# Raw tokens turned by half tiles, the inverse root behind the first product, and 16 places for expert weights

## The reference

```python
def rms_norm(x, gain):                      # eps 1e-6; rmsnorm(x, g) of the second block is the same
    xf = x.astype(jnp.float32)
    y = xf * lax.rsqrt(jnp.mean(xf * xf, axis=-1, keepdims=True) + EPS)
    return (y * gain.astype(jnp.float32)).astype(x.dtype)

def hier_moe(t, ...):                       # combine: (tokens, 32) weights, two of a row not zero
    for e in range(N_EXPERTS):
        he = jax.nn.silu(t @ w_gate[e]) * (t @ w_up[e])
        y = y + combine[:, e:e + 1] * (he @ w_down[e])

def swiglu(x, w_in, w_out):                 # D_FF = 2816
    gate, up = jnp.split(x @ w_in, 2, axis=-1)
    return (jax.nn.silu(gate) * up) @ w_out
```

## Time and profile before

| | us |
|---|---|
| median of three runs | 1882.8 |
| the runs | 1882.4, 1882.8, 1884.54 |
| the profiled execution | 1881.33 |
| its span in the trace | 1879.5 |
| PE busy in it | 1821.9 (97%) |
| DVE busy in it | 935.5 (50%) |
| ACT busy in it | 734.3 (39%) |
| POOL busy in it | 103.5 (6%) |

### The profile page before, as it was taken

The page is one execution under the profiler, slowest core; times in us unless marked ns, Lnnn a source line. Parts: engine busy times, 40 slices in busy tenths (PEclk is TensorE's granted clock), DMA queues, the critical chain, the costliest instruction groups (busy, mean ns, idle before and its releaser), DMA issues.

```text
span 1879.5 us, 30178 instructions
## 1 busy us (share of the span) xinstructions
PE 1821.9 (97%) x11760; PEld 1439.0 (77%) x11760; DVE 935.5 (50%) x1310; ACT 734.3 (39%) x1167; POOL 103.5 (6%) x113
## 2 busy tenths in 40 slices
PE   5999999999999989999999999999999999999999
PEld 3976644444434379999899998899999998879998
DVE  4873222222222165546878776554555545755554
ACT  2353212212212144444555554444444444754443
POOL 1010000000000000000212211000000000210000
PEclk9999999999999999999999999999999999999999
DMA  9876789999999976665554563566656665036653
GB/s 387 320 258 254 291 335 421 422 422 422 422 422 422 421 224 180 189 184 167 157 149 121 134 165 103 149 186 185 183 168 182 186 188 223 1 90 181 199 174 116
DMA packets 317625, 441.91 MB, mean 235 GB/s; under 512 B 11893, under 2 KB 270453, under 8 KB 289653
## 3 DMA queue, kind: packets, MB, share of 16 engines
q1 hardware_dynamic: 314728, 431.59, 66.5%
q0 software_dynamic: 2560, 8.40, 1.3%
q10 hardware_dynamic: 272, 1.05, 0.2%
HBM read 439.95 MB, written 1.05 MB: 235 GB/s over the span
## 4 chain that ended last, share of the span: by engine, by line
PE 80%; DMA 11%; DVE 5%; ACT 2%; POOL 1%; issue 1%; SPq 0%; POOLq 0%; DVEq 0%; ACTq 0%
PE PS L289 25%; PE PS L299 12%; PE PS L390 10%; DMA RAW<-w_up 9%; PE PS L2157 8%; PE PS L1740 4%; PE PS L2231 3%; PE PS L2131 2%; PE PS L166 2%; PE PS L1876 1%; PE PS L462 1%; PE PS L536 1%; PE PS L519 1%; PE PS L730 1%; PE PS L1186 1%
## 5 line engine op out<-in xcount | busy, mean ns | idle before, releaser
L289 PE MATMUL PS<-XH,LO 128*128 128x256 f32 x1344 | 380.3, 283 | 0.0
L289 PE MATMUL PS<-XL,HI 128*128 128x256 f32 x1344 | 380.3, 283 | 0.0
L289 PE MATMUL PS<-XH,HI 128*128 128x256 f32 x1344 | 379.9, 283 | 0.0
L211 DVE TENSOR_TENSOR LO<-RAW,HI 128x2048 fp32r<-128x2048 f32 x88 | 201.7, 2292 | 137.9 <-ACT HI L207 137.9
L289 PEld LDWEIGHTS PS<-XH,HI 128*128 128x128 f32 x1344 | 257.7, 192 | 3.1
L289 PEld LDWEIGHTS PS<-XL,HI 128*128 128x128 f32 x1344 | 257.7, 192 | 3.1
L289 PEld LDWEIGHTS PS<-XH,LO 128*128 128x128 f32 x1344 | 257.7, 192 | 0.0
L220 ACT ACTIVATE HI<-RAW 128x1024 fp32r<-128x1024 f32 x88 | 93.0, 1064 | 283.7 <-PE PS L299 283.7
L247 DVE TENSOR_TENSOR LO<-RAW,HI 128x1024 fp32r<-128x1024 f32 x88 | 107.5, 1225 | 185.1 <-ACT HI L220 185.1
L207 ACT ACTIVATE HI<-RAW 128x2048 fp32r<-128x2048 f32 x88 | 167.6, 1904 | 3.2 <-PE PS L1186 1.5
L299 PE MATMUL PS<-HI,HH 128*128 128x512 f32 x352 | 138.3, 393 | 0.4 <-DVE HL L255 0.2
(11 more groups left out here) (399 smaller groups left out, 3260.2 us busy)
## 6 DMA issues: line engine op xcount, KB each, us to landing
RAW<-ffn_w_in SPq DMA_DIRECT2D x176, 512.0 KB, 5.1
R<-w_gate SPq DMA_DIRECT2D x56, 1024.0 KB, 19.8
RAW<-ffn_w_out SPq DMA_DIRECT2D x88, 512.0 KB, 3.6
RAW<-a_w_in SPq DMA_DIRECT2D x69, 512.0 KB, 5.3
SPLIT<-w_up SPq DMA_DIRECT2D x31, 1024.0 KB, 22.0
RAW<-w_up SPq DMA_DIRECT2D x30, 1024.0 KB, 23.0
SPLIT<-w_down SPq DMA_DIRECT2D x30, 1024.0 KB, 17.8
R<-w_ada SPq DMA_DIRECT2D x24, 1024.0 KB, 11.3
```

What stands on the lines that cost most here:

```text
L211: v.tensor_tensor(M.LO[:, j, 0:2048], M.RAW[:, j, 0:2048], M.HI[:, j, 0:2048].bitcast(f32), ALU.subtract).then_inc(s.gu_lo[j], 1)
L289: m = e.matmul(GU[j][:, T * q:T * q + T], gu(w, j)[:, q, k, :], x[:, k, :], start=(k == 0 and n == 0), stop=(k == KT - 1 and n == 2))
```

## The change

**Norms, n = 1 to 5.** X is no longer multiplied by the root ahead of the transposes. PE turns X itself, in four steps of half a token tile (`turn(0)` to `turn(3)`), each as soon as DVE has added that part of the output; the order of the four output groups changes, so that the first 512 columns of both token tiles come first. Two of the turns stand inside the last product of the sublayer ahead, the third behind it, and the fourth inside the next first product. The matmuls of `keep_warm` go from the norms, and most of those behind the experts.

**The inverse root** is applied behind the first product. In a feed-forward layer POOL spreads each root over a 128 x 128 diagonal form (`ROW_SCALE`), PE turns it inside gate_up(1,0), and ACT copies the row of 256 roots to SBUF (`ROW`). In every half-step DVE then multiplies gate and up together by that row into a new tile GS, and Silu and H read GS. Dilated attention takes the root as a scale where ACT copies the projections, latent attention in its squares and where DVE scales the latents.

**n = 0.** The gain of the final norm is multiplied into the first gain by POOL, long before, and the tokens are turned ahead of that norm too; the X behind the norm is made later.

**Order of weights.** Between two feed-forward layers (n = 3) the second half's high part (ACT) and low part (DVE) stand ahead of the additions to X.

**Ring.** 16 places instead of 12, the loops of the expert steps written out four by four.

The core of the diff:

```diff
+    def turn(n4):
+        t, q, _ = halves(n4)
+        if n:
+            e.wait_ge(M.x_ready, 4 * n + n4 + 1)
+        elif n4 == 0:
+            e.wait_ge(M.moe.fin, 1)
+        for k in range(4 * q, 4 * q + 4):
+            m = e.transpose(TRB[k // 2][:, T * (k % 2) + 128 * t:T * (k % 2) + 128 * t + 128],
+                            X[:, t, 128 * k:128 * k + 128], M.ID[:])
+            if t and k % 2:
+                m.then_inc(M.turned, 1)
...
         late.high()
+        if after_ffn:
+            late.second_high()
+        for k in range(KT // 2):
+            high(k)
+        square(0)
+        if after_ffn:
+            square(1)
+        else:
+            a.wait_ge(M.x_ready, 4 * n + 4)
+            late.second_high()
+        for k in range(KT // 2, KT):
+            high(k)
+        if not after_ffn:
+            square(1)
+
...
     def dve():
         if n == 0:
-            v.wait_ge(M.mix.rs, 10)
+            late.first_low()
+            for k in range(KT):
+                low(k)
+            v.wait_ge(M.mix.cx_in, 32)
             for t in range(NT):
-                v.tensor_scalar(XN[:, t], M.XNF[:, t], M.RSB[:, 2 + t:3 + t], None, ALU.mult).then_inc(M.xn_done, 1)
-            late.first_low()
-        else:
-            for t in range(NT):
-                v.wait_ge(M.rstd, 4 * (n - 1) + 2 * t + 2)
-                v.tensor_scalar(XN[:, t], X[:, t], RS[:, t:t + 1], None, ALU.mult).then_inc(M.xn_done, 1)
-            late.low()
-        for k in range(KT):
-            v.wait_ge(M.xh_done, KT * n + 2 * (k // 2) + 2)
-            v.scalar_tensor_tensor(XL[:, k], TRB[k // 2][:, T * (k % 2):T * (k % 2) + T],
-                                   GC[:, g0 + k:g0 + k + 1], XH[:, k].bitcast(f32),
-                                   ALU.mult, ALU.subtract).then_inc(M.xl_done, 1)
+                v.tensor_tensor(M.XNF[:, t], X[:, t], M.NFR, ALU.mult).then_inc(M.moe.fin, 1)
+            late.second_low()
+            return
+        late.low()
+        if after_ffn:
+            late.second_low()
+        for n4 in range(3):
+            M.add[n - 1](n4)
+        for k in range(KT // 2):
+            low(k)
+        M.add[n - 1](3)
+        for k in range(KT // 2, KT):
+            low(k)
+        if not after_ffn:
+            late.second_low()
 
     def pe():
-        if n:
-            keep_warm(e, M, 5, 8)
-        for t in range(NT):
-            e.wait_ge(M.xn_done, NT * n + t + 1)
-            for k in range(KT):
-                m = e.transpose(TRB[k // 2][:, T * (k % 2) + 128 * t:T * (k % 2) + 128 * t + 128],
...
+            M.turn[n_norm](3)
     return m
 
 
...
         def silu(j, i):
-            a.wait_ge(s.gu_used[j], i + (u0 + 2))
+            a.wait_ge(s.gs_done[j], i + (u0 + 2))
             a.wait_ge(s.h_done[j], i + (u0 + 1))
-            a.activation(M.SG[:, j], GU[j][:, 0:T], ACT.Silu).then_inc(s.silu[j], 1)
+            a.activation(M.SG[:, j], M.GS[:, j, 0:T], ACT.Silu).then_inc(s.silu[j], 1)
             a.wait_ge(s.h_done[j], i + (u0 + 2))
             a.activation(M.HH[:, j], M.H[:, j], ACT.Copy).then_inc(s.hh_done[j], 1)
 
-        for j in range(2):
-            high_parts(j, 0, first=True)
+        high_parts(0, 0, first=True)
+        a.wait_ge(M.row_full, f + 2)
+        a.activation(M.ROW, PS[:, 6, 0:T], ACT.Copy).then_inc(M.row_out, 1)
+        high_parts(1, 0, first=True)
         if f == 0:
             a.wait_ge(M.x_ready, 4)
         silu(0, 0)
...
         def hidden(j, i, first=False):
+            v.wait_ge(s.gu_used[j], i + (u0 + 2))
+            if first:
+                v.wait_ge(M.row_out, f + 2)
+            v.tensor_tensor(halved(M.GS[:, j]), FIRST if first else halved(GU[j]),
+                            M.ROW.unsqueeze(1).broadcast_to([128, 2, T]), ALU.mult).then_inc(s.gs_done[j], 1)
             v.wait_ge(s.silu[j], i + (u0 + 1))
             v.wait_ge(s.dn_used[j], i + (u0 + 1))
-            v.tensor_tensor(M.H[:, j], M.SG[:, j], FIRST[1] if first else GU[j][:, T:2 * T], ALU.mult).then_inc(s.h_done[j], 1)
+            v.tensor_tensor(M.H[:, j], M.SG[:, j], M.GS[:, j, T:2 * T], ALU.mult).then_inc(s.h_done[j], 1)
             v.wait_ge(s.hh_done[j], i + (u0 + 1))
             v.tensor_tensor(M.HL[:, j], M.H[:, j], M.HH[:, j].bitcast(f32), ALU.subtract).then_inc(s.hl_done[j], 1)
 
-        gu_low(1, 0)
-        for t in range(NT if f == 0 else 0):
-            v.tensor_scalar(X[:, t], M.XNF[:, t], M.RSB[:, t:t + 1], None, ALU.mult).then_inc(M.x_ready, 2)
         for j in range(2):
             low_parts(j, 0, first=True)
+        if f == 0:
+            v.wait_ge(M.mix.rs, 10)
+            v.wait_ge(M.turned, 4)
+            v.wait_ge(M.moe.fin, 3)
+            for t in range(NT):
+                v.tensor_scalar(X[:, t], M.XNF[:, t], M.RSB[:, t:t + 1], None, ALU.mult).then_inc(M.x_ready, 2)
         hidden(0, 0, first=True)
         with v.Fori(1, FF_TWICE) as i:
...
-            v.wait_ge(s.y_done, 4 * f + n + 1)
-            xs = X[:, n // 2, 512 * (n % 2):512 * (n % 2) + 512]
-            v.scalar_tensor_tensor(xs, Y[:, n], 0.5, xs, ALU.mult, ALU.add).then_inc(M.x_ready, 1)
+
+    def add(n4):
+        t, _, cols = halves(n4)
+        v.wait_ge(s.y_done, 4 * f + n4 + 1)
+        v.scalar_tensor_tensor(X[:, t, cols], Y[:, n4], 0.5, X[:, t, cols], ALU.mult, ALU.add).then_inc(M.x_ready, 1)
+    M.add.append(add)
...
+        def turn_row():
+            e.wait_ge(M.rows_made, M.rows_before[n_norm] + NT)
+            for t in range(NT):
+                m = e.transpose(PS[:, 6, 128 * t:128 * t + 128], M.ROW_SCALE[:, t], M.ID[:])
+            m.then_inc(M.row_full, 1)
+
+        def gate_up(j, i, first=False, between=None):
             e.wait_ge(s.gu_lo[j], i + (u0 + 2))
-            e.wait_ge(s.h_done[j], i + (u0 + 1))
+            e.wait_ge(s.gs_done[j], i + (u0 + 1))
...
+                        for ahead in range(2):
+                            M.turn[n_norm + 1](ahead)
             if not last:
                 m.then_inc(s.dn_used[j], 1)
 
         gate_up(0, 0, first=True)
-        gate_up(1, 0)
+        gate_up(1, 0, between=turn_row)
         down(0, 0, first=True)
...
-    N_EARLY = LOADS + len(MORE)
-    FREED = (0, 1, 2, 3, 6, 7, 8, 9, 10, 11, 4, 5)
-    FREED_BY = (0, 1, 2, 3, 6, 7, 8, 9, 10, 11, 16, 17)
-    ring = lambda m: SLOTS[FREED[(m - len(MORE)) % LOADS]]
-    ELSEWHERE = {4: M.XH_SLOT[:], 5: M.SLOT18}
+    MORE = [M.XT2.rearrange("p k t -> p (k t)"), M.SLOT14, M.SPARE[:, 512:512 + SR], M.R_MASK[:, 5 * SR:6 * SR]]
+    FREED_BY = [n for n in range(N_EARLY) if n not in (4, 5)]
+    RING = [SLOTS[n] for n in FREED_BY if n < LOADS] + MORE + SLOTS[4:6]
+    assert len(RING) == RING_SLOTS
+    BIASES_IN, R_IN = 16 * 4, [16 * len(range(n, 31, R_SLOTS)) for n in range(R_SLOTS)]
...
+        def step_loads(i, q, r, done=0):
 
             for m in range(done, LOADS):
-                n = LOADS * (2 * i + odd) + m - N_EARLY if isinstance(i, int) and r == 0 else LOADS
-                if n < LOADS:
-                    if n % 2 == 0 and odd:
-                        sp.wait_ge(s.w_in[m // 2], 32)
-                    sp.wait_ge(s.used, FREED_BY[n] + 1)
+                n = LOADS * (PAIR_STEPS * r + q) + m
+                if isinstance(i, int) and r == 0 and 4 * LOADS * i + n < N_EARLY + RING_SLOTS:
+                    sp.wait_ge(s.used, FREED_BY[4 * LOADS * i + n - N_EARLY] + 1)
                 else:
-                    sp.wait_ge(s.used, i * (2 * LOADS) + (LOADS * (PAIR_STEPS * r + odd - 1) + m + 1))
-                load(i * 2 + odd, m)
+                    sp.wait_ge(s.used, i * (4 * LOADS) + (n - RING_SLOTS + 1))
+                load(i * 4 + q, m, n if n >= N_EARLY or (isinstance(i, int) and i == 0) else n + 4 * LOADS)
```

More of the change, by code:

```diff
@@ L50 @@
 R_SLOTS = 5
+RING_SLOTS, N_EARLY = 16, 18
 EXPERTS, N_GROUPS = 32, 4
@@ L158, in as_it_comes @@
+    def pe():
+        for n4 in range(2 if n else 0, 3):
+            turn(n4)
+    return act, pool, dve, pe, turn
 def as_it_comes(e, M, n_norm, ks, outs):
@@ L770, in pe @@
             out(n, range(KT - 1, KT)).then_inc(s.y_done, 1)
+            if n == 2:
+                for ahead in range(2):
+                    M.turn[n_norm + 1](ahead)
     def first_high(late):
@@ L2716, in _ @@
                 dve()
+            for n4 in range(4):
+                M.add[-1](n4)
         @block.tensor
```

315 lines of the change are left out of this document (180 added, 135 removed).

## The result

The changed kernel takes 1914.0 us (median of four runs, 1913.3 to 1916.0) against 1882.6: a ratio of 1.017, with a 95% interval of 1.0154 to 1.0185. It is slower, as forecast, but by 31.4 us instead of 14.5, and outside the range. The profiled execution took 1913.3 us, its span is 1911.5, 32.0 more than before.

A forecast was written before the change was run, and what follows sets the result against it. Bound by TensorE matmuls nearly everywhere, by weight loads late in the experts. Ring -8.3, loops +11.5, boundaries and end +0.95 +1.3 +1.1 +4.2 +1.0 +1.1 +0.1, clock +1.6: +14.5 on 1882.8 gives 1897.3 us, range 1886 to 1908.

The forecast's parts named there:

- the loops: Four feed-forward layers' loops: new multiplication lengthens the chain 1.10 us, 0.32 lost each iteration: +11.5 us (+3.6 to +16).
- the ring: Expert stage: 16 places close two DMA idle stretches and later weight loads move up: -8.3 us (0 to -11.3).
- the ends of the layers: Ends of feed-forward layers: last hidden product starts 2.2 us later in three layers; +0.1 us at the last.
- n=3: Boundary between two feed-forward layers: first product 0.9 us later, second 2.1, down product 7.0 behind gate's start; +4.2 us.
- n=0: Boundary behind the experts: first product starts 5.6 us earlier, but TensorE then waits 2.8 us; +0.95 us in all.
- n=5: Boundary from latent attention to feed-forward: first product 2.1 us earlier, next regular step 1.1 later; +1.1 us.
- n=2: Boundary from dilated attention to feed-forward: first product 2.1 us earlier, next regular step 1.1 later; +1.1 us.
- The clock: Boundary between two feed-forward layers: TensorE idles about 2.2 us, so one fall of the granted clock; +1.6 us.
- The one that was to end faster: Starts of layers: a short enough chain keeps the early first products' gain; 1871.8 us, chance 0.15.
- The first rival: Feed-forward loops: the slack holds, no stalls, late last products shrink by 0.8 each; 1883.5 us, chance 0.12.
- The third: Expert stage: the ring gives nothing, as SyncE or a held place keeps the bunches; 1905.6 us, chance 0.07.
- the fourth: Boundaries: the clock falls at four more of them, 1.6 us each; 1903.7 us, chance 0.08.

The follow-up runs named there:

- Experiment 1: Also written `gs_first`: changed kernel with the multiplication by the row of roots moved ahead of the down weights' low part in the feed-forward loops; 1889.2 us.
- Experiment 4: Changed kernel without the experts' further rounds, never run with these inputs: test and code left out on all engines; 1909.1 us.
- experiment 8: Changed kernel where at n=2 and n=5 VectorE waits for the two roots ahead of the second half's low part; 1916.2 us.
- ring_only: Also written experiment 2: the kernel before with only the ring's part of the change (16 places); 1877.7 us, ratio 0.9979.
- all_three: `gs_first` plus the row's copy behind the second half's weights, last hidden product before the next first low part, n=3's second low part after additions; 1882.4 us.

## Why the prediction was wrong

**The signs and the mechanisms held** in the loops, at the ring, at the ends of the layers (TensorE waits 2.3 to 2.6 us for HL at three of them, forecast some 2) and at n=3 (+4.1 for +4.2). At n=3 that is no luck: the first product came 0.8 later, the second 1.9, and the down product 7.0 behind the second, for 0.9, 2.1 and 7.0. What failed were three sizes and one assumption, all to the slow side.

**The loops, the largest part: +20.3 for +11.5.** The step that failed is "The chain grows by 1.10 us", and the stall of 0.32 from it. I took 0.08 us off the new operation, since a row on VectorE starts before the recorded end of the row ahead. But here each operation waits for another engine and none overlaps: 744.10 to 745.27 is 1.17 from the multiplication to H, and the chain grew by 1.18. That is 0.39 over the slack, and over nine iterations in four layers 14.0 us instead of 11.5. Two terms were put at nothing. TensorE, once it has stalled, takes 0.10 us to be at its pace again: its first matmul takes 0.38 us instead of 0.28, and the product behind a stall starts the next one 5.85 us later and not 5.75. With one stall at each loop's start that is 40 times 0.10, 4.0 us. The way over ScalarE's branch adds 0.8 us in the third layer and 1.5 in the last. Together 20.3. My upper end of 16 had the chain's full durations in it and neither of the other two. Experiment 1 shows that the chain is the cause of all of it: with the multiplication out of it the loops take 0.4 us more than before and not 20.3.

**n=0: +5.7 for +0.95.** The step that failed is "Now it starts 5.6 earlier". It assumed that TensorE is free as soon as the tokens are there. The earlier trace rows had an idle time of 1.6 us with no releaser, and I read it as a test of the clock only. It is a jump, which takes about as long in both kernels, and the shorter way to the first product ended at it: that product came 3.0 us earlier behind the last load, not 5.6. Experiment 4 takes the jump away: 1.7 us of the 4.7 that were missed. About 1.7 more is GpSimd: its first operation there took 0.82 and the power 2.04 us beside VectorE, where in before the same operations took 0.19 and 1.01; that this is what the regular step lost is argued from the chain of waits, not tried. The clock at half speed, which I had taken to be hidden, nearly was: the changed kernel, where it fell in the second product, takes 14.0 us from there to the regular step, and `gs_first`, where it did not, 13.8. About 1 us is not explained.

**n=5: +2.3, and n=2: +2.0, for +1.1 each.** The step that failed is "The work on GpSimd for the row is hidden: it is done some 3 us before TensorE turns it". It was written for n=3, where it held, and taken over to the starts behind attention; it was sized by GpSimd's rows in a quiet moment. The cover was gone, and TensorE waited for the row at three of the four starts (2.2 us in all, up to 1.0 each). The Trainium skill says it plainly: "GPSIMD Engine Reference", section 1 (Specifications), gives the SBUF interfaces as shared with VectorE, with contention when VectorE's instruction has two SBUF inputs. The traces agree: 0.19 us beside an addition with one operand in PSUM, 2.09 beside a subtraction of two SBUF tiles. What the delay costs each start is not shown, since in experiment 8 the wait only moved.

**The ring: -5.9 for -8.3.** In `ring_only` it is 6.7. The two differ by what lies ahead of the experts, where the code is the same: in the changed kernel the clock fell in the first gather, which took 5.3 us instead of 3.8. Counted from the end of that gather to the last load's product, the ring gives 6.4 and 6.1. The step that failed is "All later loads are at the full rate and move up by 8.3 us": I summed the idle stretches of one trace and took the two early ones as given. The two holes did close; where the other 2 us went is not explained.

**The clock: 1.6 us, at n=3.** It fell where I had said and cost nothing there, since the chain ran on VectorE and ScalarE. It fell at n=1 too, for 0.7 us, which is part of n=1's +1.7. The fall in the dilated attention that before had is missing (-1.6), and one in the latent attention is new (1.7 of its +2.4); these come and go between kernels that are the same at these places. The other 0.7 in the latent attention, which I had put at nothing, is in `gs_first` too, where the clock did not fall there; it is not explained.

**The rivals.** The one that was to end faster needed short starts; `all_three` is the nearest thing to it and ends at no change. The first rival (no stalls) fell by its own condition: the chain was to grow by at most 0.79 and grew by 1.18. The third (no gain from the ring) fell in experiment 2, and the fourth (more falls of the clock) named falls that came in part, behind the experts and at n=1 beside the one at n=3, for 0.2 us (the later of two behind the experts; what the other cost is not shown) and 0.7 us, not 1.6 each. At n=2, n=4 and n=5 the changed kernel had none, and at n=1 two kernels with the same turns had none.

## What to carry to other kernels

An operation put into a chain that crosses engines counts with its full duration and its steps, and what is over the slack is paid on every turn of the loop; the same operation, moved ahead of whatever its chain waits for, can be free. Before a step is started earlier, look at what its engine does in the time that was spare: here a jump, and an engine that is held by its neighbour, had both been hidden by the wait that the change removed. A fall of the clock has no fixed price: here one cost nothing, 0.7 or 1.9 us, by whether TensorE ended last in that stretch. Price GpSimd's operations by rows in which VectorE is busy with two SBUF operands, not by the shortest.

## What was not expected of the hardware

TensorE's idle time over a jump past a large piece of code that isn't run: 3.3 us, and none without the test and that code. The Trainium skill, "Advanced Engine Details and Errata", section ISA Cache, states that an engine keeps few lines of instructions; no run here shows that this is the reason.

GpSimd beside VectorE: 2.09 us for 0.19, 1.42 for 0.55 and 3.80 for 0.72, each ending 0.05 to 0.4 us behind VectorE's operation on two SBUF tiles.

The clock at half speed cost nothing at n=3 in the changed kernel, and 22 matmuls of no use, split by the jump, did not keep it up behind the experts (0.61 from 672 to 676).
